# Sample attention and output stage in one program, one clearing of semaphores, and operands that start alike modulo 256 bytes

## What is computed

```python
def mixer_inputs(x, pos, norm_in, w_in, q_a_norm, w_uq, kv_a_norm, w_uk):
    proj = rmsnorm(x, norm_in) @ w_in
    cq, ckv, kr, qb, kb, vb, qc, gate = jnp.split(proj, SPLIT_POINTS, axis=-1)
    q = jnp.einsum('bsr,rhd->bshd', rmsnorm(cq, q_a_norm), w_uq)
...
def mixer_output(x, o_lat, o_b, o_c, gate, w_uv, w_out):
    o_a = jnp.einsum('bshc,chd->bshd', o_lat, w_uv).reshape(B, S, MIX_A)
    o = jnp.concatenate([o_a, o_b.reshape(B, S, MIX_B), o_c.reshape(B, S, MIX_C)], axis=-1)
    return x + (o * jax.nn.silu(gate)) @ w_out
...
        xp = mixer_output(xp, o_lat, o_b, o_c, gate, w_uv[l], w_out[l])
...
        o_lat = mla_sample(ql, qr, ckv, kr, ckv_past, kr_past)
...
        xs = mixer_output(xs, o_lat, o_b, o_c, gate, w_uv[l], w_out[l])
    y_prompt = rmsnorm(xp, norm_final)
    y_sample = rmsnorm(xs, norm_final)
```

## Time and profile before

| | |
|---|---|
| median of 3 runs | 1999.72 us (1998.19 to 2001.63) |
| the profiled execution | 2000.56 us, of which the span of the core 1998.9 us |
| mean granted clock | 0.983 |
| TensorE busy | 1907.6 us, 95% of the span |
| VectorE, ScalarE, GpSimd busy | 1052.4, 891.5, 428.1 us |
| projection, TensorE's first to last product | 8 to 370 us |
| windows and memory | 378 to 564 us |
| latent projections | 568 to 689 us |
| latent attention | 694 to 1118 us |
| sample attention | 1122 to 1592 us |
| output stage | 1596 to 1991 us, span's end 1998.9 |

### The profile page before, as it was taken

How to read it: one execution, slowest core, us unless ns; L and a number is a source line. 1 busy time by engine, 2 the same in 40 slices (tenths; PEclk the granted TensorE clock), 3 DMA queues, 4 the chain that set the end, 5 groups by cost and what they waited for, 6 DMA issues and landing times. The chain is left out here.

```text
span 1998.9 us, 46161 instructions
## 1 busy us (share of the span) xinstructions
PE 1907.6 (95%) x17532; PEld 1457.0 (73%) x17532; DVE 1052.4 (53%) x3036; ACT 891.5 (45%) x2041; POOL 428.1 (21%) x567
## 2 busy tenths in 40 slices
PE   7999999799989999999999799999999799999998
PEld 6889898576768766776677566666666578888886
DVE  4433334488845466767777455555556652222232
ACT  5222222588832355556556444444443453333332
POOL 0111111245003131034011322223222231111110
PEclk9999999899999999999999899999999899999999
DMA  8434342544455420022001599777784463333331
GB/s 293 141 113 120 103 124 72 161 148 127 136 161 164 162 86 25 18 60 73 25 18 40 172 305 262 219 225 221 223 245 151 156 202 109 95 95 106 115 100 48
DMA packets 191402, 270.79 MB, mean 135 GB/s; under 512 B 37080, under 2 KB 151464, under 8 KB 182296
## 3 DMA queue, kind: packets, MB, share of 16 engines
q1 hardware_dynamic: 171560, 170.46, 29.9%
q0 software_dynamic: 19664, 97.88, 14.4%
HBM read 213.06 MB, written 54.95 MB: 134 GB/s over the span
## 5 line engine op out<-in xcount | busy, mean ns | idle before, releaser
L84 PE MATMUL proj_acc<-proj_w_hi,proj_x_hi 128*128 128x512 f32 (+2 forms) x528 | 189.1, 358 | 13.7 <-DVE proj_x_lo L343 8.2
L86 PE MATMUL proj_acc<-proj_w_hi,proj_x_lo 128*128 128x512 f32 (+2 forms) x528 | 188.1, 356 | 0.0
L85 PE MATMUL proj_acc<-proj_w_lo,proj_x_hi 128*128 128x512 f32 (+2 forms) x528 | 187.1, 354 | 0.0
L1716 ACT ACTIVATE mla_probs<-mla_probs,mla_bias 128x256 f32<-128x256 f32 (+15 forms) x128 | 153.0, 1196 | 11.5 <-DVE mla_bias L1780 7.8
L1776 DVE CUSTOM_DVE_ANT_0 mla_probs<-mla_scores,keep_in_rms 128x512 f32<-128x512 f32 x192 | 124.8, 688 | 60.7 <-PE mla_scores L1634 60.1
L2101 PE MATMUL dec_scores<-dec_keysT,sample_q_lat 128*64 128x512 f32 x512 | 123.0, 601 | 2.2 <-DVE dec_krT L2267 1.2
L84 PEld LDWEIGHTS proj_acc<-proj_w_hi,proj_x_hi 128*128 128x128 f32 x528 | 100.2, 190 | 25.3 <-issue 8.2
L2289 DVE COPY dec_pT<-dec_p_turned 128x256 f32<-128x256 f32 x80 | 34.0, 425 | 159.0 <-PE dec_outs L2117 131.2
L85 PEld LDWEIGHTS proj_acc<-proj_w_lo,proj_x_hi 128*128 128x128 f32 x528 | 99.9, 189 | 11.8
L86 PEld LDWEIGHTS proj_acc<-proj_w_hi,proj_x_lo 128*128 128x128 f32 x528 | 99.8, 189 | 11.2
L2258 DVE COPY dec_keysT<-dec_turned 128x512 f32<-128x512 f32 (+1 forms) x160 | 96.7, 646 | 17.6 <-PE dec_turned L2071 11.4
(11 more groups left out here) (437 smaller groups left out, 4913.1 us busy)
## 6 DMA issues: line engine op xcount, KB each, us to landing
win_v_tile<-wv_out SPq DMA_DIRECT2D x75, 128.0 KB
proj_x_raw<-in_xT SPq DMA_DIRECT2D x17, 512.0 KB, 5.1
proj_rows<-in_x SPq DMA_DIRECT2D x17, 512.0 KB, 3.9
featT<-proj_featT POOLq DMA_DIRECT2D x34, 256.0 KB
late_ckv<-in_xT SPq DMA_DIRECT2D x17, 512.0 KB, 6.7
late_ckv<-in_x SPq DMA_DIRECT2D x17, 512.0 KB, 3.9
y_out<-host_buf POOLq DMA_DIRECT2D x16, 512.0 KB
dec_k_rows<-in_win_k SPq DMA_DIRECT2D x64, 96.0 KB
```

The costliest lines, as they stand in the source:

```text
L84: pe.matmul(out, lh, rh, start=start, stop=False)
L85: pe.matmul(out, lh, rl, start=False, stop=False)
L86: return pe.matmul(out, ll, rh, start=False, stop=stop)
L1716: act.activation(row, row, ACT.Exp, bias=bias[:, at:at + 1], scale=-1.0, accum_out=total[:, at:at + 1]).then_inc(exp_done, 1)
```

## The change

1. Input projection: the row of weights for one k is padded from 1696 to 1728 columns (6912 bytes), the 416-column chunk moves to its end, and x's buffers are placed right behind the weights, so that x and each chunk start alike modulo 256. Each k's weights arrive in two loads, the 1280 columns of the rest and the 416 of the head; `w_pieces` counts them.
2. Latent projections: 128 bytes of padding before `cq_hi`, so that `cq` starts at 128 like `wq`.
3. Output stage: its buffers stand in another order; `wo`, `wg`, x and m all start at 64.
4. Semaphores of projection, windows and latent projections belong to `early`, which is released once, at the end of the latent projections; all others belong to `keep`, released at the end of the program. There were ten releases, there are two.
5. Sample attention and output stage are functions that return their engines' programs, and one block runs them one after the other on each engine. The first gates (`first_gates`), the splits of the gate's weights (`first_high`, `first_low`) and a first activation that loads Silu's table (`first_table`) are called from within the end of sample attention, at the places that `TAIL` gives. The four pairs of gate rows have a semaphore each. SP loads the second x tile behind pair 0, the window patterns and mix of tile 0 behind pair 2, and w_out's first four rows, behind pair 3, into the space of `keysT`. The store of the sample heads moves from SP to GpSimd, between the merges for tiles 0 and 1. Two of w_out's eight splits stand before tile 0's gated product (`OUT_AHEAD`).

```diff
+LINE = 256
+HEAD = QL + ROPE
+CHUNKS = [(KVL + 256 + 512 + 256, HEAD), (0, KVL + 256), (KVL + 256, 512), (KVL + 256 + 512, 256)]
 W_COLS = sum(n for _, n in CHUNKS)
+W_REST = W_COLS - HEAD
+W_ROW = -(-W_COLS * 4 // LINE) * LINE // 4
...
-        w_hi = b.sb("w_hi", [P, DK, W_COLS], F32R)
-        w_lo = b.sb("w_lo", [P, DK, W_COLS], F32R)
+        w_hi = b.sb("w_hi", [P, DK, W_ROW], F32R)
+        w_lo = b.sb("w_lo", [P, DK, W_ROW], F32R)
+        x_raw = b.sb("x_raw", [P, 2, DK, P])
+        x_hi = b.sb("x_hi", [P, 2, DK, P], F32R)
+        x_lo = b.sb("x_lo", [P, 2, DK, P], F32R)
...
-                first = 0 if k else HEAD
-                sp.dma_start(w_from[k % RING][:, first:], io["w_in"][k * P:(k + 1) * P, first:]).then_inc(w_loaded[k % RING], 16)
+                sp.dma_start(w_from[k % RING][:, REST_AT], io["w_in"][k * P:(k + 1) * P, HEAD:]).then_inc(w_loaded[k % RING], 16)
+                if k:
+                    sp.dma_start(w_from[k % RING][:, HEAD_AT], io["w_in"][k * P:(k + 1) * P, 0:HEAD]).then_inc(w_loaded[k % RING], 16)
...
         cq_raw = b.sb("cq_raw", [P, QK, CH])
+        b.pad("line", LINE // 2)
         cq_hi, cq_lo = (b.sb(n, [P, QK, CH], F32R) for n in ("cq_hi", "cq_lo"))
...
+        for i in range(4):
+            sp.wait_ge(pv_done, past_item[NP - 4 + i] + 1)
+            sp.dma_start(late.pairs[i], io["w_gate"][2 * i * P:(2 * i + 2) * P, :].rearrange("(k p) n -> p k n", p=P)).then_inc(late.gate_loaded[i], 16)
+            if i == X_AT:
+                output.load_second(sp)
+            if i == OUT_AT:
+                sp.wait_ge(scores_done, N)
+                for k in range(4):
+                    output.load_out(sp, k)
+            if i == MIX_AT:
+                output.load_merged(sp)
...
+        output.first_gates(pe, 0)
+        output.first_gates(pe, 1)
+        pe.wait_ge(acc_done, N)
+        pe.wait_ge(extra_read, 9)
+        swap_stats(slice(LAST, DEC_B)).then_inc(swapped, 1)
+        for k in range(2, TAIL[0]):
+            output.first_gates(pe, k)
+        pe.wait_ge(fin_link, 2 * PAST_LINKS)
+        merge(LAST, 1).then_inc(merged, 1)
+        for k in range(TAIL[0], TAIL[1]):
+            output.first_gates(pe, k)
+        pe.wait_ge(lat_kept, 2)
...
+            early.release()
```

1648 lines of the change are left out of this document (853 added, 795 removed).

## The result

Over 15 runs of each, taken in turn, the changed kernel had a median of 1990.61 us and the kernel before one of 2000.02 us; the ratio is 0.9947 (95% interval 0.9934 to 0.996). One of the 15 runs of the changed kernel took 7462.31 us; it counts in the median and not in the ratio. So the change is faster by 0.5%: 9.4 us between the medians, 10.6 by the ratio, where 23 were forecast (1977, in a range of 1970 to 1986). The profiled execution took 1989.56 us, its span 1987.9 us.

The account below looks back on a forecast made before the run. TensorE, fully busy at clock 1.00 in the input projection, latent projections and output stage, was taken as the bound; 6.5 + 3.6 + 1.2 + 2.8 + 9.3 = 23.4 us off 2000.56 gave 1977, range 1970 to 1986.

Parts of the forecast that it names:

- Part 1, output and latent projections: Output stage and latent projections: operands starting alike modulo 256 save 5.4 ns a product, 6.5 and 1.2 us.
- Part 1, projection: Input projection: operands starting alike modulo 256 save 3.6 us, bounds 0 to 5.8.
- A mean excess of 4 ns over the 390 that equal ones take: Input projection, 512-wide products: 48 a tile over 15 tiles at 4 ns each save 2.9 us.
- bounded by nothing and by 4 ns each: Input projection, 416- and 256-wide products: 720 gain between 0 and 2.9 us; a quarter, 0.7, was taken.
- Part 2, the clears: Stage boundaries: seven semaphore releases go, each saving 0.4 us of fixed cost, 2.8 us; bounds 2.0 to 4.2.
- Part 3, the joint: Sample attention's end into the output stage: first gates fill TensorE's waits, saving 9.3 us; bounds 5 to 11.4.
- That move costs nothing on the path: End of sample attention: GpSimd's split of gate row 0 before the window stores costs nothing, or 0.3 us if stores are late.
- The tail: From the last value products to the first gates' end: ends at 1599.6 instead of 1608.94, 9.3 us earlier.
- The two engines hand over to each other some four times at 0.3 us: End of sample attention: TensorE and VectorE hand-overs, some four at 0.3 us, put the first gates' end at 1599.6.
- The second rival: Sample attention's end: clock stays at half, some 20 gates take twice 0.227 us, +4.5 us, 1982; chance 0.2.
- What is late next: Output stage, third tile's gates: wait for its x tile stays about 0.3 us, up to 1.5 if VectorE slips.
- The first rival: Wide products: equal starts are worth nothing, the 5 ns stay, only 12.1 us remain, 1988; chance 0.09.

Follow-up runs that it names:

- the alignment alone: Kernel before plus 128 bytes of padding ahead of `cq_hi` in the latent projections and `x_hi` in the output stage; ratio 0.9961, 7.8 us less.
- The clears alone: Kernel before with its semaphores in two lists, released once behind the latent projections and once at the end; ratio 0.9988, 2.4 us less.
- the later split: Changed kernel with GpSimd's split of gate row 0 waiting for VectorE's last window combination, still ahead of the window stores; ratio 0.9925, 1988.48 us.
- later split, earlier swap, merge behind the shares: Changed kernel: GpSimd's gate split after VectorE's combinations, statistics swapped behind gate row 0, falls and shares sooner, GpSimd's merge waiting for shares; 1989.27 us, ratio 0.99.

## Why the forecast was wrong

**Part 1, output and latent projections: right.** 6.5 and 1.2 us were forecast; the alignment alone gave 7.8 of 7.7. In the changed kernel the latent products gained their 1.1 us too, but the stage opened 0.7 us later and closed with 0.3 us more idle, so that its row in the table shows 0.1; the opening was not tested. The comparison inside the kernel before, same shape, same moving operand, two places, was worth as much as an experiment.

**Part 1, projection: wrong, 0.6 instead of 3.6.** Two steps failed. "A mean excess of 4 ns over the 390 that equal ones take" took the 390 of one kind as what all three would come to; in the changed kernel L98 (high x high) stays at 396 and the mean falls by 2. And the narrower products were "bounded by nothing and by 4 ns each": a loss was left out without a reason. The 256-wide ones lost 3 to 5 ns in duration. The measured 0.6 lies within the term's own bounds of 0 to 5.8; the value taken in them was too high.

**Part 2, the clears: right mechanism, and 2.8 us within what was measured.** The clears alone gave 2.4 us (0.4 to 4.4). In the changed kernel the idle at the three boundaries fell by 0.9, 0.6 and 0.8 us and the end by 0.3; the release behind the latent projections, which clears the semaphores of three stages at once, makes that one 0.3 us longer (4.47 to 4.78 us before the first product of latent attention), where the forecast had it 0.4 shorter. Together that is 2.3 us.

**Part 3, the joint: wrong by its smallest line.** "That move costs nothing on the path" was said of GpSimd's split of gate row 0, and it cost 3.8 us. The step looked at who waits for the split and for the stores, and not at who works beside it. The combinations it now ran beside have two operands in SBUF, and the earlier trace rows, 1457 against 1287 ns beside GpSimd's merge, had already shown what that does; the forecast applied it to the splits of the tail alone. It is the rule of the Trainium skill, "SBUF — State Buffer", section "Who interferes with whom", that such a VectorE instruction collides with GpSimd's reads, and there the trace agrees beyond what the earlier trace rows showed: short instructions suffer most, as they last until GpSimd's is done (0.47 to 2.45 us and 0.16 to 1.26), while those of 1024 columns go from 1.29 to 1.46 in the mean.

**The tail: the first gates were to end at 1599.6 and ended at 1605.5.** 2.9 of these 5.9 us were there before the tail began. Of its 9.3 us, 6.3 came in, and of the missing 3.0 the later split gives back 0.8 (22.8 to 22.0 us). "The two engines hand over to each other some four times at 0.3 us" was the step: the swap stood behind gate row 1, whose low part VectorE makes behind its last accumulation, then the falls waited for the swap, the shares for a third split, each of them stretched by the merge, and TensorE waited 2.71 us at once. The second rival (the clock at half) had its place right and its price in part: the eight products from 1595.41 to 1598.74 took 3.33 us, 1.5 more than at 0.227 each, and the two value batches before lost 1.1 us each. With the long waits gone (later split, earlier swap, merge behind the shares) the clock stayed at 1.00 and the tail took 18.1 us, 1.6 less than forecast. So the low clock was met only together with the waits; it is not shown that a wait of a given length brings it.

**What is late next: not seen.** The forecast allowed up to 1.5 us for the third tile's x; TensorE has no idle there in the changed kernel.

The range missed because its bounds were drawn round each term as if the terms that cost nothing had no bounds; the split's line had one of 0.3 us, and cost 3.8. The first rival (alignment worth nothing, 1988) is near the measured time by luck: its mechanism is refuted by the kernel with the alignment alone.

## What to carry to other kernels

When work moves to another time on GpSimd, list what VectorE does at that time, and let each of its short instructions with two SBUF operands last until GpSimd's instruction beside it is done (here up to 2.0 us more each); where there is a choice, start the GpSimd work on a semaphore that says VectorE's short chain is done. In a tail where several engines take turns, put the instructions that others wait for (the swap, the shares) ahead of bulk work even if they are short: with that order the tail fell from 22.0 us to 18.1 to 21.2, by what GpSimd did beside it. And where two kinds of the same product stand in one profile at different places in memory, their difference is a measured price for that width; for another width it isn't, and can have the other sign.
